# The pool's fp32 products replaced by products of rounded halves

## The chip, the cores and the metric

The kernel runs on one core of a Trainium2 chip. The metric is device time in microseconds of one execution, as the median of several. The engines named here are TensorE (PE; its weight loads are listed as PEld), VectorE (DVE), ScalarE (ACT) and SyncE (SP), which issues most transfers.

## What is computed

A decoder trunk of two residual layers on 256 tokens of 2048 features, all in float32. Layer 0 has a parallel attention and retention mixer, layer 1 a pooling mixer; each layer ends in a gated MLP with a short convolution, and a last norm follows. The change touches the pooling mixer of layer 1 alone:

```
h = rms_norm(x, mix_norm[1])
for group gi, window w in ((0, 2), (1, 4), (2, 8), (3, 16)):      # 512 channels each
    pooled_g[s] = mean(h_g[max(0, s-w+1) .. s]) - h_g[s]          # over min(s+1, w) tokens
    y_g = pooled_g @ pool_w[gi]                                   # 512 x 512
x = x + y * pool_scale
```

The trailing mean minus the token itself is a linear map over the 256 tokens, so it is a product with a fixed 256 x 256 matrix per group, the pool matrix. It is zero above the diagonal and more than w - 1 below it; only its first w columns (tokens that have fewer than w predecessors, the ramp) hold fractions other than 1/w; all the others hold 1/w and 1/w - 1, where w is a power of two.

## The kernel before

**Weight products.** Every weight matrix is streamed once from memory in units of 512 rows by 512 columns, four tiles of 128 rows each, into four slots `raw`. For accuracy a float32 product is made of three products of rounded halves: ScalarE writes the rounded value (`hi`, w_hi, L854), VectorE the remainder (`lo` = raw - hi, w_lo, L1265), and TensorE multiplies hi by the high half of the activation, lo by the same, and hi by the activation's low half (`token_unit`, L606, L608, L609). One unit is 24 products with 512 moving columns. `hi` and `lo` hold one unit, so ScalarE may round tile kt of the next unit only after TensorE is done with tile kt of this one (`w_used`), and a tile of `lo` follows its `hi` tile. The two elementwise engines have their other work written between these tiles by hand, at fixed places (`between`, called after each tile kt).

**The pool.** The map over tokens is applied after the channel product. TensorE takes units U_POOL + 0 to 3, one for each group; the result of group g, z_g, is 256 tokens (two tiles of 128 partitions) by 512 features in two PSUM banks. ScalarE copies it out and scales each token by its norm (`project_out`, L1091, one operation of 512 elements for each token tile, signal `z_ready`). Then `pool_tokens(g)` multiplies it by the pool matrix: for each of four blocks m of 128 features one fp32 product of token tile 0 with the first 128 + w columns of the matrix (L785), and one of token tile 1 with the last 128 (L787), both summed in the same two banks. VectorE adds the result times `pool_scale` to x (`pool_out`, L1693), in four operations. The tile of the matrix in SBUF, `pool_m`, has 384 columns for each group: 256 of the first 128 tokens, and 128 of the others.

**Order.** TensorE: units 0, 1, a small sum of squares (L622), unit 2, pool group 0, unit 3, pool groups 1 and 2, then the first up unit (`up`, first waits until `pool_out(1)` is done), pool group 3, the second up unit. ScalarE: hi of unit 1 with `last_squares` between (four `h` roundings, L860, at its end), hi of unit 2, the root of the squares, `project_out(0)`, hi of unit 3 with `project_out(1)` between, `project_out(2)`, hi of the first up unit with `first_h` between, `project_out(3)`, a square, then the `h` roundings of group 1 once `pool_out(1)` is done. VectorE: lo of unit 2, lo of unit 3, `pool_out(0)`, lo of the first up unit with the low half of `h` between (L1300), `pool_out(1)`, `pool_out(2)`, lo of the second up unit, `pool_out(3)`.

`z_of` (L191) gives the four groups' z the space of `yv`, `yg`, `u` and `yv` again, so `project_out(3)` waits for pool group 0 (`pooled_mm`). `act` (44 tiles by 512 elements, rounded type) holds the MLP's activations and isn't in use between the last down unit of layer 0 and the second window of the up products of layer 1.

Of the kernel before, what the change touches and what calls it, by code (L numbers as in the profile page):

```python
# [23 lines left out]
ALU = mybir.AluOpType  # L24
ACT = mybir.ActivationFunctionType
AX = mybir.AxisListType
F32 = mybir.dt.float32
F32R = mybir.dt.float32r

P = 128  # L30
# [5 lines left out]
KT = 4  # L36


def trunk_kernel(nc, xT, rel_bias, norm_g, w_in, w_out, lam, subln, pool_w, pool_scale,
                 w_up, conv, w_down, bucket_onehot, rot_cos, rot_sin, decay, pool_matrix, ident_in, flip_in, outT):  # L40
    D, S = xT.shape
# [80 lines left out]
    TURN = 32  # L122
    TAIL = 3
    NORM_AT = (1, 0)
    NEAR = [P + w for w in POOL_WINDOWS]

    ctx = ExitStack()
    with ctx:
# [59 lines left out]
        u = sb("u", [P, 4, S])  # L188
        yv = sb("yv", [P, 4, S])
        yg = sb("yg", [P, 4, S])  # L190
        z_of = [t.rearrange("p (t k) s -> p t (k s)", t=2) for t in (yv, yg, u, yv)]  # L191
        ps = ctx.enter_context(nc.psum_tensor("ps", [P, 8, 512], F32))

        def sem(name):
            return ctx.enter_context(nc.semaphore(name))
# [73 lines left out]
        gated = sem("gated")  # L269
        act_hi = sem("act_hi")  # L270
        act_lo = sem("act_lo")
        z_ready = sem("z_ready")
        pooled_mm = sem("pooled_mm")
        weighted = sem("weighted")
        x_rows = sem("x_rows")
# [211 lines left out]
        def _(pe):  # L487
# [286 lines left out]
            for l in range(DEPTH):  # L774
                if l == 1:
                    def pool_tokens(g):

                        pe.wait_ge(z_ready, 2 * (g + 1))
                        if g == 0:
                            pe.wait_ge(table_in, 16 * N_TABLE)  # L780
                        z, b = z_of[g], POOL_BANKS[g]
                        for m in range(4):
                            c = slice(m * P, (m + 1) * P)
                            out = ps[:, b + m // 2, (m % 2) * S:(m % 2 + 1) * S]
                            pe.matmul(out[:, 0:NEAR[g]], z[:, 0, c], pool_m[:, g, 0:NEAR[g]], start=m % 2 == 0, stop=False,  # L785
                                      skip_group_check=True)
                            mm = pe.matmul(out[:, P:2 * P], z[:, 1, c], pool_m[:, g, S:S + P], start=False, stop=True,  # L787
                                           skip_group_check=True)
                        mm.then_inc(pooled_mm, 1)

                    for g in range(4):
                        if g == 0:
                            pe.wait_ge(evacuated, G_POOL - 1)
                        if g == 2:
                            pe.wait_ge(evacuated, G_POOL)
                        if g == 3:
                            pe.wait_ge(rms_done, 3)

                        def pool_h(kt):
                            pe.wait_ge(h_lo, H_BASE[2] + KT * g + kt + 1)  # L800
                        token_unit(U_POOL + g, ps[:, POOL_BANKS[g]:POOL_BANKS[g] + 2, :], True, True, g, pool_h)
                        if g == 1:
                            sum_squares(2, POOL_BANKS[3] + 1)
                        if g >= 2:
                            pool_tokens(g - 2)
                    pool_tokens(2)

                def up(i, first):
                    for gt in range(2):
                        G = G_UP[l] + gt  # L810

                        pe.wait_ge(evacuated, i * 2 + G - (2 if first and gt == 0 and l == 1 else 1))
                        for j in range(UP_UNITS):
                            def split(kt):
                                pe.wait_ge(h_lo, H_BASE[2 * l + 1] + KT * j + kt + 1)
                            token_unit(U_UP[l] + 4 * gt + j, ps[:, wide_bank(G):wide_bank(G) + 2, :], j == 0,
                                       j == UP_UNITS - 1, j, split if first and gt == 0 else None, base=i * (8 * KT))
                            if first and l == 1 and gt == 0 and j == 0:
                                pool_tokens(3)
                            if first and gt == 1 and j == 0:  # L820
                                sum_squares(2 * l + 1, wide_bank(G_UP[l]) + 3)

                up(0, True)
                pe.wait_ge(rms_done, 2 * l + 2)
                with pe.Fori(1, PAIRS) as i:
                    up(i, False)
                for g in range(DN_GROUPS):
                    G = G_DN[l] + g
                    pe.wait_ge(evacuated, G - 1)
                    for j in range(DN_UNITS):  # L830
                        n, whole = U_DN[l] + DN_UNITS * g + j, j == DN_UNITS - 1
                        pe.wait_ge(act_lo, l * PAIRS + j + 1)
                        if l == 1 and g == DN_GROUPS - 1 and j == DN_UNITS - TAIL:
                            pe.wait_ge(act_lo, (l + 1) * PAIRS)
                            tail_units(n, ps[:, wide_bank(G):wide_bank(G) + 2, :], wide_bank(G + 1))
                            break
                        if l == 1 or g < DN_GROUPS - 1:
                            token_unit(n, ps[:, wide_bank(G):wide_bank(G) + 2, :], j == 0, whole, j, None, act)
                        else:
                            wide_unit(n, 0, wide_bank(G), j == 0, whole, lambda kt: act[:, KT * j + kt, :], None, opening(j))  # L840
# [3 lines left out]
        def _(sc_e):  # L844
# [238 lines left out]
            for l in range(DEPTH):  # L1083
                if l == 1:
                    def project_out(g, ts=range(2)):

                        sc_e.wait_ge(w_used, KT * (U_POOL + g + 1))
                        if g == 3:
                            sc_e.wait_ge(pooled_mm, 1)
                        for t in ts:  # L1090
                            a_.activation(z_of[g][:, t, :], ps[:, POOL_BANKS[g] + t, :], ACT.Copy,  # L1091
                                          scale=rstd[:, S + t:S + t + 1]).then_inc(z_ready, 1)

                    def last_squares(kt):
                        if kt == 1:
                            sc_e.wait_ge(evacuated, G_DN[0] + 4)
                            square(2, 3)
                        if kt == 3:
                            h_round(2, 3, 2)

                    def first_out(kt):
                        if kt == 0:
                            project_out(1, [0])
                        if kt == 1:
                            project_out(1, [1])

                    def first_h(kt):
                        if kt == 0:
                            sc_e.wait_ge(evacuated, G_POOL + 1)
                            h_round(3, 0, 3)  # L1110

                    w_hi(U_POOL, 0, 0, 16 * (R_POOL[0] + 1))
                    w_hi(U_POOL + 1, 0, 1, 16 * (R_POOL[1] + 1), last_squares)
                    w_hi(U_POOL + 2, 0, 2, 16 * (R_POOL[2] + 1))
                    root(2, POOL_BANKS[3] + 1)
                    sc_e.wait_ge(rstd_ready, 3)
                    project_out(0)
                    w_hi(U_POOL + 3, 0, 3, 16 * (R_POOL[3] + 1), first_out)
                    project_out(2)
# [140 lines left out]
        def _(ve):  # L1260
# [424 lines left out]
            for l in range(DEPTH):  # L1685
                if l == 1:
                    def pool_out(g):

                        ve.wait_ge(pooled_mm, g + 1)
                        b = POOL_BANKS[g]  # L1690
                        for m in range(4):
                            t = 4 * g + m
                            last = ve.scalar_tensor_tensor(x[:, t, :], ps[:, b + m // 2, (m % 2) * S:(m % 2 + 1) * S],  # L1693
                                                         pscale[:, t:t + 1], x[:, t, :], ALU.mult, ALU.add)
                        last.then_inc(evacuated, 1)

                    w_lo(U_POOL, 0, 0)
                    add_down(0, 3)
                    w_lo(U_POOL + 1, 0, 1, between=lambda kt: fold_last(kt - 1))
                    h_lo_group(2, 3, 2)  # L1700
                    w_lo(U_POOL + 2, 0, 2, kts=range(3))
                    invert(2)
                    w_lo(U_POOL + 2, 0, 2, kts=[3])
                    w_lo(U_POOL + 3, 0, 3)
                    pool_out(0)

                def v_windows(i, peel):
                    q = i * 2 + (l * 2 * PAIRS - 1)
                    for j in range(UP_UNITS):
# [6 lines left out]
                        if peel:  # L1716
                            if l == 0 and j == 0:
                                add_mixed(3)
                            if l == 0 and j == 3:
                                add_squares(1, 3)  # L1720
                            if l == 1 and j == 0:
                                pool_out(1)
                                pool_out(2)
                            if l == 1 and j == 1:
# [237 lines left out]
```

## Time and profile before

| | us |
|---|---|
| median of 3 runs | 1913.1 (1912.54 to 1913.1) |
| the profiled execution | 1912.37 |
| its span, first to last instruction | 1910.1 |
| TensorE busy in it | 1901.6 |
| VectorE busy | 1406.6 |
| ScalarE busy | 1064.0 |
| the pool's fp32 products, first to last start | 1166.97 to 1185.17 |

The times of the profile are microseconds from the start of the span. The granted TensorE clock is full throughout. A matmul's duration in the trace includes its way through the array, and consecutive ones overlap: what a product costs a busy TensorE is the distance between two starts.

### The profile page before, as it was taken

The page shows a single profiled execution, that of the slowest core. Times are in us where ns is not written, and L with a number is a line of the kernel's source. Part 1 is how long each engine was busy: PE and PEld are TensorE (multiplying, and loading weights), DVE is VectorE, ACT ScalarE, POOL GpSimd, SP SyncE. Part 2 cuts the span into 40 slices and gives each one's busy share as a digit, 9 for nine tenths or more (in the row PEclk, how much of TensorE's full clock was granted, in tenths as well). Part 3 has the DMA queues.
Part 4 walks back from the last instruction along what each step waited for, and adds up shares of the span by engine and source line. Part 5 has one row for each costly group of instructions (what it writes and reads, how often), then busy time and mean ns, then how long its engine had stood idle before and what let it go on. Part 6 is the DMA issues. An engine that isn't in the chain of part 4 may idle for free.

```text
span 1910.1 us, 26860 instructions
## 1 busy us (share of the span) xinstructions
PE 1901.6 (100%) x8654; PEld 1579.6 (83%) x8654; DVE 1406.6 (74%) x2287; ACT 1064.0 (56%) x1792; POOL 50.5 (3%) x54
## 2 busy tenths in 40 slices
PE   9999999999999999999999999999999999999998
PEld 8888888888888888888888888888888888888887
DVE  6666867777777777877766677777787777766665
ACT  7545544566555555555554556555555655555544
POOL 0000522000000000000000000000000000000000
PEclk9999999999999999999999999999999999999999
DMA  8845645575877777786665555677877777756653
GB/s 284 285 157 192 208 160 165 208 249 192 250 245 240 236 236 245 244 241 214 220 220 189 188 175 178 229 238 229 249 246 243 233 235 246 239 186 200 218 198 110
DMA packets 231984, 416.26 MB, mean 218 GB/s; under 512 B 13635, under 2 KB 54124, under 8 KB 231916
## 3 DMA queue, kind: packets, MB, share of 16 engines
q1 hardware_dynamic: 199804, 369.82, 59.4%
q10 hardware_dynamic: 32112, 45.55, 8.1%
q8 instruction: 41, 0.67, 0.2%
q14 instruction: 27, 0.22, 0.0%
HBM read 383.85 MB, written 24.13 MB: 214 GB/s over the span
## 4 chain that ended last, share of the span: by engine, by line
PE 98%; DVE 1%; ACT 0%; issue 0%; DVEq 0%
PE ps L606 29%; PE ps L609 29%; PE ps L608 29%; PE ps L498 4%; PE ps L502 2%; PE ps L570 1%; DVE lo L1265 0%; PE ps L585 0%; PE ps L574 0%; PE ps L589 0%; PE ps L593 0%; PE ps L541 0%; PE ps L543 0%; PE ps L542 0%; PE ps L720 0%; PE ps L785 0%
## 5 line engine op out<-in xcount | busy, mean ns | idle before, releaser
L1265 DVE TENSOR_TENSOR lo<-raw,hi 128x512 fp32r<-128x512 f32 x1352 | 919.6, 696 | 469.3 <-ACT hi L854 457.1
L854 ACT ACTIVATE hi<-raw 128x512 fp32r<-128x512 f32 x1336 | 830.8, 630 | 772.2 <-PE ps L609 706.4
L606 PE MATMUL ps<-hi,h 128*128 128x512 f32 x1824 | 714.8, 392 | 0.3 <-DVE lo L1265 0.2
L609 PE MATMUL ps<-hi,h 128*128 128x512 f32 x1824 | 710.3, 389 | 0.0
L608 PE MATMUL ps<-lo,h 128*128 128x512 f32 x1824 | 709.8, 389 | 0.0
L606 PEld LDWEIGHTS ps<-hi,h 128*128 128x128 f32 x1824 | 342.4, 188 | 74.6 <-DVE lo L1265 4.9
L609 PEld LDWEIGHTS ps<-hi,h 128*128 128x128 f32 x1824 | 342.3, 188 | 72.0
L608 PEld LDWEIGHTS ps<-lo,h 128*128 128x128 f32 x1824 | 342.5, 188 | 70.1
L606 PE MATMUL ps<-hi,act 128*128 128x512 f32 x592 | 230.5, 389 | 0.0
L609 PE MATMUL ps<-hi,act 128*128 128x512 f32 x592 | 230.3, 389 | 0.0
L608 PE MATMUL ps<-lo,act 128*128 128x512 f32 x592 | 230.3, 389 | 0.0
L606 PEld LDWEIGHTS ps<-hi,act 128*128 128x128 f32 x592 | 111.1, 188 | 23.5 <-issue 0.5
L609 PEld LDWEIGHTS ps<-hi,act 128*128 128x128 f32 x592 | 111.1, 188 | 23.2
L608 PEld LDWEIGHTS ps<-lo,act 128*128 128x128 f32 x592 | 111.1, 188 | 23.0
L1057 ACT ACTIVATE yg<-u,cw 128x256 f32<-128x256 f32 x88 | 52.0, 590 | 17.4 <-DVE u L1634 17.4
L498 PE MATMUL ps<-act,hi 128*128 128x512 f32 x176 | 60.8, 394 | 0.0
L1057 ACT ACTIVATE yv<-u,cw 128x256 f32<-128x256 f32 x88 | 51.9, 590 | 14.0 <-DVE u L1634 14.0
L1634 DVE TENSOR_TENSOR u<-sqacc,rstd 128x512 f32<-128x512 f32 x84 | 54.0, 684 | 0.0
L1623 DVE STREAM_TRANSPOSE sqt<-ps 128x1024 f32<-128x1024 f32 x42 | 52.2, 1243 | 0.0
L502 PE MATMUL ps<-act,lo 128*128 128x256 f32 x176 | 48.1, 277 | 0.0
L1878 POOL TENSOR_TENSOR x<-x,rstd 128x512 f32<-128x512 f32 x2 | 2.6, 1280 | 1606.7 <-ACT rstd L1239 1606.7
L1669 DVE STREAM_TRANSPOSE u<-ps 32x256 f32<-32x256 f32 x96 | 42.8, 446 | 2.9
(207 smaller groups left out, 1179.8 us busy)
## 6 DMA issues: line engine op xcount, KB each, us to landing
raw<-in_w_up SPq DMA_DIRECT2D x176, 1024.0 KB, 5.7
raw<-in_w_down SPq DMA_DIRECT2D x88, 1024.0 KB, 5.1
raw<-in_w_in SPq DMA_DIRECT2D x52, 1024.0 KB, 7.0
turned_rows<-sqt ACTq DMA_DIRECT2D x42, 512.0 KB, 5.9
sqacc<-turned_rows ACTq DMA_DIRECT2D x168, 128.0 KB, 6.1
raw<-in_w_out SPq DMA_DIRECT2D x16, 1024.0 KB, 7.4
raw<-in_w_in SPq DMA_DIRECT2D x16, 256.0 KB, 5.3
sqacc<-sqt SPq DMA_DIRECT2D x128, 32.0 KB, 1.9
```

Source lines behind the costliest of these rows:

```text
L498: pe.matmul(ps[:, bank + m, :], hi[:, kt, m * P:(m + 1) * P], mv, start=first and kt == 0, stop=False, skip_group_check=True)
L502: return pe.matmul(ps[:, bank + m, S:2 * S], lo[:, kt, m * P:(m + 1) * P], mv[:, 0:S], start=False, stop=last and kt == KT - 1, skip_group ...
L570: pe.matmul(acc[:, m, :], hi[:, kt, c], mv, start=first and kt == 0 and a == 0, stop=False, skip_group_check=True)
L606: pe.matmul(acc[:, t, :], xh, hi[:, kt, :], start=first and kt == 0, stop=False, skip_group_check=True)
L608: pe.matmul(acc[:, t, :], xh, lo[:, kt, :], start=False, stop=False, skip_group_check=True)
L609: mm = pe.matmul(acc[:, t, :], xl, hi[:, kt, :], start=False, stop=last and kt == KT - 1, skip_group_check=True)
L854: a_.activation(out[:, kt, :], raw[:, slot, kt, :], ACT.Copy).then_inc(hi_done, 1)
L1057: a_.activation(y[:, m, :], u[:, m, :], ACT.Identity, scale=cw[:, l, bass.ds(t, 1), 2], bias=cw[:, l, bass.ds(t, 1), 3]).then_inc(y0, 1)
L1265: ve.tensor_tensor(halves[1][:, kt, :], raw[:, slot, kt, :], halves[0][:, kt, :].bitcast(F32), ALU.subtract).then_inc(lo_done, 1)
L1623: ve.transpose(turned_u.rearrange("p (q k s) -> p q k s", q=4, k=8), rows).then_inc(evacuated, 1)
L1634: scaled = ve.tensor_tensor(out, quads, r, ALU.mult)
L1669: ve.transpose(cols, rows).then_inc(x_turned, 1)
```

## The change

The z of each group is split into rounded halves. ScalarE rounds z out of the bank into `z_hi` (same operation as before, other output type and place, signal `z_rounded`), and VectorE computes z - z_hi out of the same bank into `z_lo` (`project_low`, signal `z_ready`). The pool matrix is rounded as a whole into `pool_hi`; a remainder `pool_lo` is made for the first 16 columns of each group, the ramp. All four lie in `act`. Each of the four feature blocks then has five products of rounded operands instead of two of fp32: z_hi and z_lo by the near columns, z_hi by the ramp's remainder (16 columns), z_hi and z_lo by the far columns.

```diff
+    RAMP = max(POOL_WINDOWS)
-        z_of = [t.rearrange("p (t k) s -> p t (k s)", t=2) for t in (yv, yg, u, yv)]
+        z_hi = [act[:, 2 * g:2 * g + 2, :] for g in range(4)]
+        z_lo = [act[:, 8 + 2 * g:8 + 2 * g + 2, :] for g in range(4)]
+        pool_hi = act[:, 16:19, :].rearrange("p a b -> p (a b)").rearrange("p (g c) -> p g c", g=4)
+        pool_lo = act[:, 19, 0:4 * RAMP].rearrange("p (g c) -> p g c", g=4)
...
                         pe.wait_ge(z_ready, 2 * (g + 1))
                         if g == 0:
-                            pe.wait_ge(table_in, 16 * N_TABLE)
-                        z, b = z_of[g], POOL_BANKS[g]
+                            pe.wait_ge(pool_split, 1)
+                        zh, zl, b = z_hi[g], z_lo[g], POOL_BANKS[g]
                         for m in range(4):
...
-                            pe.matmul(out[:, 0:NEAR[g]], z[:, 0, c], pool_m[:, g, 0:NEAR[g]], start=m % 2 == 0, stop=False,
+                            pe.matmul(out[:, 0:NEAR[g]], zh[:, 0, c], pool_hi[:, g, 0:NEAR[g]], start=m % 2 == 0, stop=False,
                                       skip_group_check=True)
-                            mm = pe.matmul(out[:, P:2 * P], z[:, 1, c], pool_m[:, g, S:S + P], start=False, stop=True,
+                            pe.matmul(out[:, 0:NEAR[g]], zl[:, 0, c], pool_hi[:, g, 0:NEAR[g]], start=False, stop=False,
+                                      skip_group_check=True)
+                            pe.matmul(out[:, 0:RAMP], zh[:, 0, c], pool_lo[:, g, :], start=False, stop=False,
+                                      skip_group_check=True)
+                            pe.matmul(out[:, P:2 * P], zh[:, 1, c], pool_hi[:, g, S:S + P], start=False, stop=False,
+                                      skip_group_check=True)
+                            mm = pe.matmul(out[:, P:2 * P], zl[:, 1, c], pool_hi[:, g, S:S + P], start=False, stop=True,
                                            skip_group_check=True)
...
                     def project_out(g, ts=range(2)):
                         sc_e.wait_ge(w_used, KT * (U_POOL + g + 1))
-                        if g == 3:
-                            sc_e.wait_ge(pooled_mm, 1)
                         for t in ts:
-                            a_.activation(z_of[g][:, t, :], ps[:, POOL_BANKS[g] + t, :], ACT.Copy,
-                                          scale=rstd[:, S + t:S + t + 1]).then_inc(z_ready, 1)
+                            a_.activation(z_hi[g][:, t, :], ps[:, POOL_BANKS[g] + t, :], ACT.Copy,
+                                          scale=rstd[:, S + t:S + t + 1]).then_inc(z_rounded, 1)
...
                     w_hi(U_POOL + 1, 0, 1, 16 * (R_POOL[1] + 1), last_squares)
+                    sc_e.wait_ge(w_used, KT * U_POOL)
+                    a_.activation(pool_hi[:, :, :], pool_m[:, :, :], ACT.Copy).then_inc(pool_rounded, 1)
                     w_hi(U_POOL + 2, 0, 2, 16 * (R_POOL[2] + 1))
...
+                    def project_low(g, ts=range(2)):
+                        for t in ts:
+                            ve.wait_ge(z_rounded, 2 * g + t + 1)
+                            ve.scalar_tensor_tensor(z_lo[g][:, t, :], ps[:, POOL_BANKS[g] + t, :], rstd[:, S + t:S + t + 1],
+                                                    z_hi[g][:, t, :].bitcast(F32), ALU.mult, ALU.subtract
+                                                    ).then_inc(z_ready, 1)
...
                     w_lo(U_POOL + 2, 0, 2, kts=[3])
-                    w_lo(U_POOL + 3, 0, 3)
+                    ve.wait_ge(pool_rounded, 1)
+                    ve.tensor_tensor(pool_lo[:, :, :], pool_m[:, :, 0:RAMP], pool_hi[:, :, 0:RAMP].bitcast(F32),
+                                     ALU.subtract).then_inc(pool_split, 1)
+                    project_low(0)
+                    w_lo(U_POOL + 3, 0, 3, between=lambda kt: project_low(1, [kt - 2]) if kt > 1 else None)
                     pool_out(0)
+                    project_low(2)
...
                             if l == 1 and j == 0:
+                                project_low(3)
                                 pool_out(1)
                                 pool_out(2)
```

## Rows read from the trace of the kernel before

**Rows 1.** The page: busy time of TensorE, and the chain that ended last, by engine.
```profile
PE 1901.6 (100%) x8654; PEld 1579.6 (83%) x8654; DVE 1406.6 (74%) x2287; ACT 1064.0 (56%) x1792; POOL 50.5 (3%) x54
PE 98%; DVE 1%; ACT 0%; issue 0%; DVEq 0%
```

**Rows 2.** Timeline of TensorE: start, length, line, operands, count of records merged.
```profile
1147.71 0.39 PE L498 MATMUL ps<-act,hi 128*128 128x512 f32 x1
1149.79 0.39 PE L498 MATMUL ps<-act,hi 128*128 128x512 f32 x1
...
1166.97 0.38 PE L785 MATMUL ps<-pool_m,yv 128*128 128x130 f32 x2
1168.98 0.40 PE L608 MATMUL ps<-lo,h 128*128 128x512 f32 x1
1173.98 0.39 PE L609 MATMUL ps<-hi,h 128*128 128x512 f32 x1
1174.21 0.39 PE L785 MATMUL ps<-pool_m,yg 128*128 128x132 f32 x2
1176.00 0.40 PE L785 MATMUL ps<-pool_m,u 128*128 128x136 f32 x2
1177.60 0.38 PE L787 MATMUL ps<-pool_m,u 128*128 128x128 f32 x2
1178.25 0.40 PE L608 MATMUL ps<-lo,h 128*128 128x512 f32 x1
1183.53 0.41 PE L785 MATMUL ps<-pool_m,yv 128*128 128x144 f32 x2
1185.63 0.40 PE L608 MATMUL ps<-lo,h 128*128 128x512 f32 x1
```

**Rows 3.** Timeline of TensorE's weight loads around the sum of squares, 1160.3 to 1162.2.
```profile
1160.80 0.64 PEld L622 LDWEIGHTS ps<-ones,sqacc 128*128 128x128 f32 x4
1161.35 0.19 PEld L606 LDWEIGHTS ps<-hi,h 128*128 128x128 f32 x1
1161.46 0.19 PEld L608 LDWEIGHTS ps<-lo,h 128*128 128x128 f32 x1
1161.71 0.19 PEld L609 LDWEIGHTS ps<-hi,h 128*128 128x128 f32 x1
```

**Rows 4.** Timeline of ScalarE, 1148 to 1196; in brackets idle time before and releaser.
```profile
1154.24 1.06 ACT L889 ACTIVATE sqt<-x 128x1024 f32<-128x1024 f32 x1 [0.55 <-DVE x L1683]
1155.20 1.21 ACT L854 ACTIVATE hi<-raw 128x512 fp32r<-128x512 f32 x2
1156.32 1.70 ACT L860 ACTIVATE h<-x,gains 128x256 fp32r<-128x256 f32 x4
1157.92 1.21 ACT L854 ACTIVATE hi<-raw 128x512 fp32r<-128x512 f32 x2
...
1161.22 0.63 ACT L854 ACTIVATE hi<-raw 128x512 fp32r<-128x512 f32 x1 [0.73 <-PE ps L609]
...
1174.94 1.25 ACT L1091 ACTIVATE yv<-ps,rstd 128x512 f32<-128x512 f32 x2
...
1177.89 1.71 ACT L860 ACTIVATE h<-x,gains 128x256 fp32r<-128x256 f32 x4 [0.76 <-DVE x L1693]
```

**Rows 5.** Timeline of VectorE, 1148 to 1196.
```profile
1156.54 0.42 DVE L1291 TENSOR_TENSOR sqt<-sqt 128x256 f32<-128x256 f32 x1
...
1162.12 0.67 DVE L1265 TENSOR_TENSOR lo<-raw,hi 128x512 fp32r<-128x512 f32 x1
1164.05 0.69 DVE L1265 TENSOR_TENSOR lo<-raw,hi 128x512 fp32r<-128x512 f32 x1 [1.26 <-ACT hi L854]
...
1168.95 1.66 DVE L1693 SCALAR_TENSOR_TENSOR x<-ps,pscale,x 128x256 f32<-128x256 f32 x4 [0.43 <-PE ps L787]
...
1175.78 0.47 DVE L1300 SCALAR_TENSOR_TENSOR h<-x,gains,h 128x256 fp32r<-128x256 f32 x1
1176.20 1.66 DVE L1693 SCALAR_TENSOR_TENSOR x<-ps,pscale,x 128x256 f32<-128x256 f32 x4
```

More of the change, by code:

```diff
@@ L271, in trunk_kernel @@
         act_lo = sem("act_lo")
+        z_rounded = sem("z_rounded")
         z_ready = sem("z_ready")
+        pool_rounded = sem("pool_rounded")
+        pool_split = sem("pool_split")
         pooled_mm = sem("pooled_mm")
```

## The prediction

> **What bounds the kernel now.** I read the page's busy shares and its chain of waits first [rows 1]: TensorE is busy for 1901.6 of 1910.1 us and 98% of the chain that ended last is TensorE work. So a change counts by the TensorE time it adds or removes, and by whether it makes TensorE wait. Next, TensorE in order of time around the pool [rows 2]. A product of the four-group pool is one `matmul` in fp32 and stands in the trace as two records ("x2"). Group 0 runs from 1166.97; the second product of the following weight unit starts at 1168.98, so its first began to stream one interval (0.227, below) earlier, at 1168.755: group 0 holds TensorE for 1.785 us. Group 1: 1174.21 to 1176.00, 1.79 us. Group 2: eight starts from 1176.00 to 1177.60 are seven intervals of 0.2286, so it ends at 1177.83, 1.83 us. Group 3: 1183.53 to 1185.63 less 0.227, that is 1185.40, 1.87 us. Sum 7.275 us for 32 products. After group 2 the next unit's second product starts at 1178.25, its stream at 1178.02: TensorE stood still for 0.19 us. `up` waits there for `pool_out(1)`, which VectorE ran from 1176.20 for 1.66 us, to 1177.86 [rows 5]; the wait reaches TensorE 0.16 us later.
>
> **The price of a product in halves.** The new products have operands of rounded type (as all weight products have) with 128 to 144 moving columns, and 16 for the ramp. None so short is in the trace. What is there: 512 columns every 0.227 us (1168.98 to 1173.98, 22 intervals), and the pair of a 512 and a 256 column product every 0.347 (1147.71 to 1149.79, six pairs), so 0.119 for 256 [rows 2]. Both are columns over 2.4 GHz plus 0.013, so 128 would stream in 0.066: that is the lower end, if nothing else limits. The upper end is the fp32 product itself, 0.223 (1.785 / 8), if short rounded products get no faster path. What decides is the stationary operand: each product loads its own. Where the moving side is one column, in the sum of squares before unit 2, the loads show what they take alone [rows 3]: four of them end with one that starts at 1160.80 + 0.64 - 0.19 = 1161.25, then come the loads of two rounded products at 1161.35 and 1161.46. That is 0.10 to 0.11 apart, and 0.11 between the two rounded ones, with almost no streaming beside the first; the following load, behind a 512-column stream, comes 0.25 later. A load overlaps the stream before it, so a product costs the longer of 0.11 and its stream. I take 0.11 for all five kinds, also for the 16 columns of the ramp.
>
> Per group: four blocks by five products (near high, near low, ramp, far high, far low) = 20 products x 0.11 = 2.20 us, where eight fp32 products took about 1.8. Four groups: 80 x 0.11 = 8.80 against 7.275: **+1.53 us** of TensorE. Forty-eight more products, each cheaper by half only.
>
> Beside this rule of the trace stands one of the Trainium skill (TensorE: Matmul & The Clock Gate, section "Back-to-back issue gap"), which speaks for a shorter spacing: in a stream of load and product pairs with 128 columns it gives about 81 ns each. By it a group would be an estimated 1.62 us and the four 6.5. No row here has such a pair; the loads in [rows 3] are 0.10 to 0.11 apart, so I go by these.
>
> **ScalarE.** Added: `pool_hi`, one Copy of 4 x 384 = 1536 elements per partition. A 1024-element ScalarE operation occupies 0.96 (1154.24 to the next at 1155.20), a 512-element one 0.58, so 1536 is about 1.4 us [rows 4]. It stands between the `h` roundings that end at 1158.0 and the `hi` tiles of unit 2, from 1157.92 before. These move to 1159.3, 1159.9 and 1160.5; the fourth waits for TensorE until 1161.22 as before [rows 4]. VectorE's `lo` of the first tile then ends at about 1160.6, and unit 2 begins at 1161.38: hidden, by 0.7 us. If that cover were gone it would cost up to 1.4. The eight `z` copies stay as they are, into other memory; the wait of `project_out(3)` for `pooled_mm` goes, and is worth nothing: at 1174.94 pool group 0 had been done for 6 us.
>
> **VectorE.** Added: `pool_lo`, 64 elements, about 0.2, and eight subtractions of 512 elements out of the bank. The near rows are four `x<-ps` operations of 256 elements in 1.66 us, 0.40 apart, and a 512-element operation lasts 0.69 where a 256-element one lasts 0.42: 0.27 for 256 elements more, so about 0.66 each [rows 5]. Bounds 0.60 and 0.80 (twice 0.40). In sum 5.3 us, and where they stand decides:
> - `pool_lo` and `project_low(0)` follow the `lo` tile at 1162.12: 1162.8, then 1162.9 to 1164.25. They delay the first `lo` of unit 3 from 1164.05 to 1164.25; TensorE wants it at 1169.2. Group 0 starts on time at 1166.97.
> - `project_low(1)` goes between tiles at 1167.1 and 1168.5: free, wanted at 1174.6.
> - Group 0 now ends at 1169.17, so unit 3, the ScalarE tiles behind it and `pool_out(0)` (1168.95 before [rows 5], now 1169.37 to 1171.0) are 0.415 later. `project_low(2)` runs to 1172.3, and the four pairs of `lo` and `h` low half behind it catch up: the last one waits for ScalarE's fourth tile again and ends at 1176.6 instead of 1176.2.
> - `project_low(3)` stands ahead of `pool_out(1)`. Its inputs are ready at 1176.05 and 1176.6, it runs 1176.6 to 1177.92. Then `pool_out(1)`: 1177.92 to 1179.58, and 0.16 later, at 1179.74, TensorE may start the first `up` unit. TensorE itself is through with group 2 at 1174.625 + 4.40 = 1179.03. It stands still for 0.71 us, where it was 0.19: **+0.52 us**. Queued behind on VectorE: `pool_out(2)` until 1181.2, and on ScalarE the `h` roundings of group 1, from 1179.6 (1177.89 before) and then the tiles of the second `up` unit, from 1182.2; TensorE wants those at 1187.4, so they are free.
>
> Group 3 stands between `up` units 0 and 1, its `z_ready` came at 1177.9. Nothing later in the kernel is nearer to a limit than before, so the loss isn't given back: 1.53 + 0.52 = **+2.05 us**. The profiled execution took 1912.37, its span of 1910.1 and 2.27 around it; it would become 1914.4. The median of the three runs is 1913.1 (1912.54 to 1913.1), 0.7 above the profiled one: I forecast **1915.2**. That is 0.11%, less than the 0.2% (3.8 us) that a measurement of this kernel tells from no change.
>
> **The rivals.**
> A, short products stream freely (0.066, the ramp 0.02): a group is 16 x 0.066 + 4 x 0.02 = 1.14 us. For it: the law of the 512 and 256 rows. Against it: [rows 3]. It doesn't bring 4 x 0.67 = 2.7 us, because VectorE takes the place of TensorE: `pool_out(0)` can't start before `project_low(1)` is through at 1169.1, `project_low(2)` ends at 1172.0, the four pairs of 1.0 us run without a gap to 1176.06, `project_low(3)` to 1177.4, `pool_out(1)` to 1179.04. The first `up` unit starts at 1179.2 instead of 1178.02, +1.2, and group 3 gives 0.7 back: +0.5, 1913.6. (By the 81 ns of the skill's page the same chain holds, and group 3 gives 0.25 back: an estimate of 1914.0.)
> B, on the other side: rounded products under 256 columns run at the fp32 pace. For it: nothing in the trace is shorter than 256, exactly where the stream (0.119) meets the load (0.11), and the two differ by operand type only. Against it: there is one record per rounded product and two per fp32 product. A group is 16 x 0.223 + 4 x 0.11 = 4.0 us; TensorE is then the later one and the stall of 0.19 goes: 16.0 - 7.275 - 0.19 = +8.5, 1921.6, slower by 0.44%. It decides from 0.14 us a product on.
> C, load and stream of short products don't overlap: 0.11 + 0.066 = 0.176 and 0.13 for the ramp, 3.3 a group, 13.3 - 7.275 - 0.19 = +5.9, 1919.0. Against it: the fp32 records overlap their loads already.
> D, the forecast with the `pool_hi` copy uncovered, +1.4: 1916.6. Against it, 0.7 us of slack at the first tile and more at each later one.
>
> **How the numbers follow.** Forecast 0.62, A (with the 81 ns case) 0.14, B 0.11, C 0.07, D 0.06. Range: down past A and the spread of the runs, 1912.9; up past D and to C, 1919.3; left out are B and the edges, under 0.2. Slower by over 0.2%, beyond 1916.9: B, C and the edge of D and of the forecast (a subtraction of 0.80 adds 0.14 x 2 on the way to `pool_out(1)`), 0.20. Faster by over 0.2% needs -3.8, more than A's whole TensorE saving: 0.02. Within: 0.78.
>
> **What would show it.** The 80 products start 0.11 apart, whatever their columns; 0.066, 0.176 or 0.22 speaks for A, C, B. The groups take 2.2 us each. The stop before the first `up` unit is about 0.7 us and ends with `pool_out(1)`. The `pool_hi` row lies near 1158 to 1159.4 with no gap on TensorE at 1161.4. The subtractions take about 0.66 apart. It would be wrong if TensorE had a stop at group 0 or 1, waiting for `z_ready` or `pool_split`, or if the difference lay anywhere outside 1160 to 1190.

## The result, and the profile after

The changed kernel takes 1915.37 us as the median of 22 executions, beside 1912.89 of 22 of the kernel before: a ratio of 1.0015, with a 95% interval of 1.0009 to 1.0021. That is 2.5 us more: the interval excludes equality, the ratio lies inside the 0.2% that was set as the bound of "no change", and the interval's upper end just past it. The forecast was 1915.2.

The 22 executions stand in two groups: 13 from 1914.56 to 1915.45 (middle 1915.02), nine from 1916.37 to 1917.45 (middle 1916.70). The profiled one, 1916.78, is of the upper group; its span is 1914.5. A second profile of the same kernel, from the lower group, follows with the first experiment.

TensorE at the end of unit 2, in pool group 0 and behind it, as in [rows 2]. Each product is one record now, and its length is modelled; what counts is the distance from five products to the next five (0.50 for the first five of group 0, 0.56 for the next).

```profile
1167.35 0.39 PE L616 MATMUL ps<-hi,h 128*128 128x512 f32 x1
1167.58 0.22 PE L792 MATMUL ps<-act 128*128 128x130 f32 x1
1167.63 0.28 PE L794 MATMUL ps<-act 128*128 128x130 f32 x1
1167.75 0.22 PE L796 MATMUL ps<-act 128*128 128x16 f32 x1
1167.83 0.31 PE L798 MATMUL ps<-act 128*128 128x128 f32 x1
1167.97 0.27 PE L800 MATMUL ps<-act 128*128 128x128 f32 x1
1168.08 0.28 PE L792 MATMUL ps<-act 128*128 128x130 f32 x1
...
1170.04 0.40 PE L615 MATMUL ps<-lo,h 128*128 128x512 f32 x1
...
1175.26 0.22 PE L792 MATMUL ps<-act 128*128 128x132 f32 x1
1177.44 0.28 PE L792 MATMUL ps<-act 128*128 128x136 f32 x1
...
1179.56 0.28 PE L800 MATMUL ps<-act 128*128 128x128 f32 x1
1180.25 0.50 PE L613 MATMUL ps<-hi,h 128*128 128x512 f32 x1 [0.41 <-DVE x L1706]
1180.59 0.56 PE L615 MATMUL ps<-lo,h 128*128 128x512 f32 x1
1180.95 0.63 PE L616 MATMUL ps<-hi,h 128*128 128x512 f32 x1
1181.37 0.63 PE L613 MATMUL ps<-hi,h 128*128 128x512 f32 x1
...
1187.42 0.23 PE L792 MATMUL ps<-act 128*128 128x144 f32 x1
1189.89 0.40 PE L615 MATMUL ps<-lo,h 128*128 128x512 f32 x1
```

Read it as [rows 2] were read. Group 0 holds TensorE from 1167.58 to 1170.04 - 0.227 = 1169.81, group 1 from 1175.26 to 1177.44, group 2 to 1179.56 + 0.11 = 1179.67, group 3 from 1187.42 to 1189.66: 2.23 + 2.18 + 2.23 + 2.24 = 8.88 us, where it was 7.275. Then the stop, from 1179.67 to 1180.59 - 0.227 = 1180.36: 0.69 us, where it was 0.19. Then something that the forecast doesn't have: the products of the first up unit follow each other every 0.427 us instead of 0.227, from about 1181 to 1184, and the unit takes 1180.36 to 1187.42, 7.06 us; before it was 1178.02 to 1183.53, 5.51 us. The stretches of this profile say why (columns: stretch, its length, busy time of PE, PEld, DVE, ACT, POOL, granted clock, DMA share, GB/s):

```profile
1174.00:1179.00 5.00, 5.00 (x41) 4.77 (x40) 4.77 (x10) 3.47 (x6) 0.00 (x0) 1.00 0.18 38
1181.00:1184.00 3.00, 3.00 (x9) 2.33 (x8) 1.15 (x3) 2.51 (x5) 0.00 (x0) 0.50 0.09 34
1184.00:1187.00 3.00, 3.00 (x15) 2.47 (x14) 1.86 (x5) 1.77 (x4) 0.00 (x0) 0.99 0.00 0
```

The granted clock is 0.50 in 1181 to 1184: TensorE ran at 1.2 GHz instead of 2.4 right behind the thin products and the stop. So this execution lost 1.61 us to the products, 0.50 to the stop and 1.55 to the clock, 3.66 in all. The spans differ by 4.4. Of the rest, 0.61 is there before anything of the change has run: the small sum of squares ahead of unit 2 starts at 1161.63 where it was 1161.02, and VectorE is as much later at 1152.33, before the `pool_hi` copy. That is no effect of the change: in the traces of the twelve experiments below the same sum starts anywhere from 1160.88 to 1161.89, and the two that are the kernel before up to there have 1161.49 and 1161.89.

VectorE and ScalarE, which answer to [rows 4, 5]: `pool_hi` (L1126), the subtractions (L1714) and `pool_out` (L1706).

```profile
1158.53 1.47 ACT L1126 ACTIVATE act<-pool_m 128x1536 fp32r<-128x1536 f32 x1
1159.91 1.65 ACT L867 ACTIVATE hi<-raw 128x512 fp32r<-128x512 f32 x3
```
```profile
1160.55 1.89 DVE L1278 TENSOR_TENSOR lo<-raw,hi 128x512 fp32r<-128x512 f32 x3 [0.47 <-ACT hi L867]
...
1163.31 0.22 DVE L1726 TENSOR_TENSOR act<-pool_m,act 128x64 fp32r<-128x64 f32 x1
1163.56 1.41 DVE L1714 SCALAR_TENSOR_TENSOR act<-ps,rstd,act 128x512 fp32r<-128x512 f32 x2
...
1177.23 1.40 DVE L1714 SCALAR_TENSOR_TENSOR act<-ps,rstd,act 128x512 fp32r<-128x512 f32 x2
1178.55 3.21 DVE L1706 SCALAR_TENSOR_TENSOR x<-ps,pscale,x 128x256 f32<-128x256 f32 x8
```

The copy of 1536 elements holds ScalarE for 1.38 us. The tiles of `hi` behind it come late by that, and TensorE doesn't wait for them: the first `lo` tile of unit 2 is written from 1160.55 to about 1161.24, TensorE begins that unit at about 1162.1. Two subtractions take 1.32 from the first start to what follows, 0.66 each. `project_low(3)` stands from 1177.23 to 1178.55 ahead of `pool_out(1)`, which ends 1.66 later, at 1180.2; TensorE goes on at 1180.36.

### The profile page after: what moved, and what is told of

The parts are those of the page before. It is cut to its first block, busy times and chain, and to the rows that moved or that the text cites. A ratio compares the mean times of both kernels' runs of the same rounds, so it can differ in the third digit from the quotient of the medians.

```text
span 1914.5 us, 26901 instructions
## 1 busy us (share of the span) xinstructions
PE 1905.4 (100%) x8670; PEld 1583.1 (83%) x8670; DVE 1412.8 (74%) x2296; ACT 1065.2 (56%) x1793; POOL 50.4 (3%) x54
## 4 chain that ended last, share of the span: by engine, by line
PE 98%; DVE 1%; ACT 1%; issue 0%; DMA 0%; DVEq 0%; ACTq 0%
PE ps L613 29%; PE ps L616 29%; PE ps L615 29%; PE ps L505 4%; PE ps L509 2%; PE ps L577 1%; DVE lo L1278 1%; PE ps L592 0%; PE ps L596 0%; PE ps L581 0%; PE ps L600 0%; PE ps L548 0%; PE ps L550 0%; PE ps L549 0%; PE ps L645 0%; PE ps L712 0%
```

## The experiments

All times below are medians. The experiments ran in three sets, each beside the kernel before on the same chip: the first four, where the kernel before had 1912.95 (33 executions); the next four, 1912.93 (28); and the last three with the second run of the longer stop, 1913.27 (29). Theory 1 and theory 2 of the expectations are stated in the first of them. "Over before" is over the kernel before of the same set.

**The changed kernel again.** No edit.

> The changed kernel itself, run again beside the others for a direct comparison. Theory 1 (80 products at 0.11 us, and a stop of about 0.7 us before the first up unit behind project_low(3) and pool_out(1)): 2.0 to 2.8 us over the kernel before. Theory 2, to which its profile gave rise: in some executions TensorE's granted clock falls to 1.2 GHz for about 3.4 us after that stop, which adds another 1.7 us, so that the times come in two groups, near 1914.9 and near 1916.6.

1915.17 of 11, ratio 1.0012 (1.0003 to 1.0021), 2.2 over before. Nine executions from 1914.44 to 1915.42, two at 1916.23 and 1916.43: two groups again. Its profile is of the lower group. TensorE there, around the stop:

```profile
1179.44 0.28 PE L800 MATMUL ps<-act 128*128 128x128 f32 x1
1180.14 0.50 PE L613 MATMUL ps<-hi,h 128*128 128x512 f32 x1 [0.42 <-DVE x L1706]
1180.48 0.40 PE L615 MATMUL ps<-lo,h 128*128 128x512 f32 x1
1180.72 0.40 PE L616 MATMUL ps<-hi,h 128*128 128x512 f32 x1
```

The same stop (1179.55 to 1180.25, 0.70), and products every 0.23 behind it. So these two profiles differ by whether the clock falls behind the stop. For all other executions the record has only the mean granted clock of the whole, which such a fall takes to 0.999. It is 0.999 in ten of the eleven upper executions of the 33 and 1.000 in one (1916.51), which must be high for another reason. In 14 of the 22 lower ones it is 1.000; 0.998 or 0.999 in the other eight doesn't tell a fall here, because the clock is also low at the very end of the kernel (in this profile, whose mean is 0.998, in the last 6 us alone).

**Without the stop.**

```diff
-pe.wait_ge(evacuated, i * 2 + G - (2 if first and gt == 0 and l == 1 else 1))
+pe.wait_ge(evacuated, i * 2 + G - (3 if first and gt == 0 and l == 1 else 1))
```

> The changed kernel, with the first up unit waiting for pool_out(0) in place of pool_out(1); the banks it writes are group 0's. TensorE then doesn't stop between pool group 2 and the first up unit, and nothing else is touched. Theory 1: 0.7 us less than the lower group of the changed kernel, near 1914.3, that is 1.5 over before. Theory 2, the stop is what lets the clock fall: all executions in one group, so 1 to 1.5 less in the median of a sample with both. Rival (the thinly streaming products alone bring the clock down, whatever the stop): two groups again, 1.7 apart.

1914.23 of 11, ratio 1.0008 (0.9999 to 1.0017): 0.94 less than the changed kernel beside it, 0.8 less than that one's lower group. Ten executions lie from 1913.73 to 1914.72, one at 1915.75, whose mean granted clock is 1.000. In its profile the first up unit follows group 2 at once:

```profile
1179.01 0.28 PE L800 MATMUL ps<-act 128*128 128x128 f32 x1
1179.13 0.45 PE L613 MATMUL ps<-hi,h 128*128 128x512 f32 x1
1179.41 0.40 PE L615 MATMUL ps<-lo,h 128*128 128x512 f32 x1
```

**`project_low(3)` behind `pool_out(1)`.**

```diff
                             if l == 1 and j == 0:
-                                project_low(3)
                                 pool_out(1)
+                                project_low(3)
                                 pool_out(2)
```

> The changed kernel with project_low(3) behind pool_out(1) in VectorE's order; the wait of the first up unit as it was. If it is this order that makes the stop, pool_out(1) ends 1.3 us earlier, ahead of pool group 2's end, and the result is that of the relaxed wait: near 1914.3, one group. If the stop came from elsewhere (the later end of unit 3, the four lo and h pairs), some 0.2 to 0.7 us of it stays.

1914.24 of 11, ratio 1.0007 (0.9997 to 1.0016), all from 1913.72 to 1914.91. Its profile:

```profile
1177.74 1.66 DVE L1706 SCALAR_TENSOR_TENSOR x<-ps,pscale,x 128x256 f32<-128x256 f32 x4 [0.33 <-PE ps L800]
1179.32 1.40 DVE L1714 SCALAR_TENSOR_TENSOR act<-ps,rstd,act 128x512 fp32r<-128x512 f32 x2
```
```profile
1179.66 0.28 PE L800 MATMUL ps<-act 128*128 128x128 f32 x1
1179.78 0.45 PE L613 MATMUL ps<-hi,h 128*128 128x512 f32 x1
```

`pool_out(1)` now waits for TensorE and not the other way round, and the stop is gone. It was the place of two subtractions in VectorE's order that made it. What the two kernels without a stop have left over the kernel before, 1.3 us, is the products: 1.61 in the profile, less the 0.19 of the old stop, is 1.42.

**The kernel before with the relaxed wait.** The same edit of the wait, in the kernel before.

> The kernel before with the same relaxed wait alone. Theory 1: its stop of 0.19 us goes, 0.2 us less than before (1912.7), and the profile shows the first up unit right behind pool group 2. Rival (the 0.19 us is how rounded products start behind fp32 products, not a wait): nothing changes.

1912.95 of 11, equal to before (ratio 0.9999, 0.9990 to 1.0008). In the profile the 0.19 us are gone (group 2 ends at 1178.69, the next unit's stream starts at 1178.68), but 0.2 us is less than 11 executions tell; the median neither confirms it nor denies it.

**Without the ramp products.** The kernel without the stop, less these:

```diff
-pe.matmul(out[:, 0:RAMP], zh[:, 0, c], pool_lo[:, g, :], ...)
```

> The kernel without the stop (relaxed wait of the first up unit), and without the 16 products by the ramp's remainder; the pool's first 16 tokens then lose what rounding takes from fractions like 1/3. Theory 1, a product costs its weight load, 0.111 us, however few its columns: 16 x 0.111 = 1.78 us less, near 1912.5, and the groups take 1.78 us each. Rival, 16 columns cost what they stream (0.02 us): 0.3 us less, near 1913.9.

1912.66 of 11, 1.57 less than without the stop (1.64 less than the next kernel, of the same set), 0.27 less than before (ratio 1.0000, 0.9991 to 1.0009). Sixteen products of 16 columns cost nearly what theory 1 says (1.78), and five times what they would if streaming were their price. One block of group 2:

```profile
1176.87 0.28 PE L792 MATMUL ps<-act 128*128 128x136 f32 x1
1176.98 0.28 PE L794 MATMUL ps<-act 128*128 128x136 f32 x1
1177.10 0.27 PE L796 MATMUL ps<-act 128*128 128x128 f32 x1
1177.20 0.28 PE L798 MATMUL ps<-act 128*128 128x128 f32 x1
1177.32 0.28 PE L792 MATMUL ps<-act 128*128 128x136 f32 x1
```

Four products in 0.45, five took 0.56 (1178.56 to 1179.12 in the changed kernel's group 2).

**A ramp of 128 columns.**

```diff
-    RAMP = max(POOL_WINDOWS)
+    RAMP = P
```

> The kernel without the stop, with the remainder of the pool matrix kept for 128 columns in place of 16, so that all 80 products have 128 or more moving columns; VectorE's pool_lo has 512 elements in place of 64. Theory 1: the same time as with 16 columns (1914.2 within 0.3), because 128 columns stream in 0.066 us behind a load of 0.111. Rival, streams add to loads: 16 x 112 columns / 2.4 GHz = 0.75 us more, near 1915.0.

1914.30 of 11, ratio 1.0008 (0.9999 to 1.0017), where 16 columns gave 1914.23 in the set before. One of the 11 executions took 4091.77 us, the only one of its kind in the record; why isn't known, and the median doesn't depend on it. Eight times the columns cost nothing: in the profile the loads are 0.11 apart as before, and 16 x 112 more columns stream behind them.

**A longer stop behind thin products, twice.**

```diff
-pe.wait_ge(evacuated, i * 2 + G - (2 if first and gt == 0 and l == 1 else 1))
+pe.wait_ge(evacuated, i * 2 + G - 1)
```

> The changed kernel with a longer stop: the first up unit waits for pool_out(2) too. The stop grows from 0.7 to about 2.2 us behind the rounded products. Theory 2 (stop and thinly streaming products together let the clock fall): 1.6 us over the changed kernel's lower group for the stop, and in more executions than there another 1.7 us: two groups near 1916.6 and 1918.3, most in the upper. Rival (the falls have nothing to do with the stop): one in five to one in two in the upper group, as before.

> The changed kernel with the longer stop once more, for the counts. Theory 2: at least half of the executions near 1918.3 (clock at 1.2 GHz for a while behind the stop), against two of eleven behind fp32 products with a stop of the same length. Rival, the kinds of product don't matter: as few as there.

1918.56 of 6 (ratio 1.0033, 1.0021 to 1.0045) and 1918.10 of 7 (1.0028, 1.0016 to 1.0039). No execution of the 13 is near 1916.6; the lowest is 1917.61. The two profiles show the fall, for the others it is read from their times: without it they would lie near 1916.5 (the changed kernel's lower group and 1.5 for the longer stop). The first has a stop of 2.16 us and the low pace from the first product on:

```profile
1179.36 0.28 PE L800 MATMUL ps<-act 128*128 128x128 f32 x1
1181.63 0.63 PE L613 MATMUL ps<-hi,h 128*128 128x512 f32 x1 [2.00 <-DVE x L1706]
1182.06 0.63 PE L615 MATMUL ps<-lo,h 128*128 128x512 f32 x1
```

The second has a stop of 2.25 us, four products at the full pace behind it, and the low one from the fifth or sixth on:

```profile
1181.07 0.50 PE L613 MATMUL ps<-hi,h 128*128 128x512 f32 x1 [1.98 <-DVE x L1706]
...
1182.45 0.63 PE L616 MATMUL ps<-hi,h 128*128 128x512 f32 x1
```

**The same stop behind fp32 products.** The same edit in the kernel before.

> The kernel before with the same longer wait: a stop of about 2.0 us in place of 0.19, behind fp32 products, which keep the array streaming. In both theories 1.8 us more for the stop, near 1914.75. If the thin products are needed for the clock to fall, one group; if a stop of 2 us does it by itself, another 1.7 us in a part of the executions, near 1916.4.

1914.90 of 11, ratio 1.0010 (1.0001 to 1.0019): 1.97 over before. Nine executions lie from 1914.31 to 1915.02; their middle is 1.73 over before, which is the stop (from 1178.30 to 1180.32, 2.02 us where it was 0.19, 1.83 more). Two are at 1916.09 and 1916.49. The profiled one is the latter, and has the low clock too, from about the sixth product on:

```profile
1180.20 0.50 PE L606 MATMUL ps<-hi,h 128*128 128x512 f32 x1 [1.75 <-DVE x L1693]
1180.55 0.40 PE L608 MATMUL ps<-lo,h 128*128 128x512 f32 x1
...
1181.80 0.63 PE L606 MATMUL ps<-hi,h 128*128 128x512 f32 x1
```

So behind a stop of 2 us the clock falls in two of 11 executions after fp32 products (one seen in a profile, one by its time) and in all 13 after the rounded ones. Theory 2 is borne out: falls come with the stop, and more often with the rounded products before it; "at least half" was too timid. One difference is left untested: the stops behind the rounded products were 0.14 to 0.23 us longer than the one behind fp32 products.

**A ramp product with 32 stationary columns.**

```diff
-pe.matmul(out[:, 0:RAMP], zh[:, 0, c], pool_lo[:, g, :], ...)
+pe.matmul(out[0:TURN, 0:RAMP], zh[:, 0, m * P:m * P + TURN], pool_lo[:, g, :], ...)
```

> The kernel without the stop, in which the 16 ramp products load 32 of their block's 128 features as stationary columns; the ramp's remainder is left out for the other 96. Theory 1, the 0.111 us is the time of loading 128 stationary columns: 32 take about a quarter, 0.03, a ramp product costs 0.03 to 0.05 and the sum is 1.0 to 1.3 us less than without the stop (1914.2), near 1913.1. Rival, 0.111 is what any product costs that comes with a load, whatever its size: nothing changes, 1914.2.

1913.71 of 11, ratio 1.0003 (0.9994 to 1.0012). The kernel with all 128 columns that ran beside it (next) had 1914.56, so 0.85 less. Loads and what follows them, in its profile:

```profile
1175.53 0.19 PEld L794 LDWEIGHTS ps<-act 128*128 128x128 f32 x1
1175.64 0.11 PEld L796 LDWEIGHTS ps<-act 128*32 128x32 f32 x1
1175.70 0.19 PEld L798 LDWEIGHTS ps<-act 128*128 128x128 f32 x1
1175.81 0.19 PEld L800 LDWEIGHTS ps<-act 128*128 128x128 f32 x1
```

Behind a load of 128 columns the next comes 0.11 later, behind one of 32 columns 0.06. Neither the proportional price (0.03) nor the fixed one (0.11): the price of a thin product falls with its stationary columns, to something near 0.06. The Trainium skill (TensorE: Matmul & The Clock Gate, section "LDWEIGHTS (loading the stationary operand)") gives the number of stationary columns divided by 1.2 as a load's nanoseconds: an estimated 107 ns for 128 and 27 ns for 32. The trace's 0.11 agrees with the first, its 0.06 is twice the second. The same page of the Trainium skill, in "Wait — 56ns, not 53.3ns?", has about 62 ns of sequencer time for each matmul in one of its modes. The 0.06 is near that; which mode this chip runs no trace here shows, so what sets the 0.06 is open.

**Two products in a row with one stationary operand.** The ramp product moved ahead of the z_lo product.

> The kernel without the stop, with the ramp product moved next to the near product of the same high half, so that two products in a row have the same stationary operand. Theory 1: each product loads its own, 80 loads, nothing changes (1914.2 within 0.3). Rival, an equal stationary operand isn't loaded again: up to 16 x 0.09 = 1.4 us less.

1914.56 of 11, ratio 1.0005 (0.9996 to 1.0014). The profile has a load ahead of every product, 0.11 apart. Nothing is saved by the order.

**The whole result without ramp products.** The matrix's ramp columns are stored as multiples of 1/w, `pool_lo` goes, and VectorE corrects 64 results a group:

```diff
...
+ramp = ps[:, b:b + 2, :].rearrange("p a (h s) -> p (a h) s", h=2)[:, :, 0:RAMP]
+factors = pool_m[:, g, S + P:S + P + RAMP].unsqueeze(1).to_broadcast([P, 4, RAMP])
+ve.tensor_tensor(ramp, ramp, factors, ALU.mult).then_inc(pool_split, 1)
+ve.wait_ge(pool_split, g + 1)
...
```

> A version with the whole result and without the ramp products: the matrix's first w columns are held as multiples of 1/w, which the rounded type holds exactly, and VectorE multiplies the ramp's 16 results of each block by w/(s+1) in the bank, one operation of 64 elements a group, ahead of pool_out. 64 products of 0.111 us, no stop, pool_lo gone. Theory 1: as without the ramp, near 1912.7, level with the kernel before (16 loads of halves cost the same as 16 records of fp32). Rival: the four operations on the bank and their waits (0.3 to 0.4 each) come on the path of pool_out and stop TensorE again, up to 1 us more.

1912.78 of 11, beside 1913.27 of before; ratio 0.9999 (0.9990 to 1.0008). The correction takes 0.22 us and puts `pool_out` off by 0.26:

```profile
1178.39 0.22 DVE L1703 TENSOR_TENSOR ps<-ps,pool_m 128x64 f32<-128x64 f32 x1
1178.65 1.66 DVE L1707 SCALAR_TENSOR_TENSOR x<-ps,pscale,x 128x256 f32<-128x256 f32 x4
```

It is level with the kernel before and no faster. Of the versions tried that keep the whole result, this is the fastest in halves; that none could be faster with z as the stationary operand isn't shown.

## Why the prediction was right

**A product costs its load, 0.11 us: shown.** The forecast had 8.80 us, the profile 8.88; +1.53 forecast, +1.61 measured. That it is the load and not the stream is shown from three sides: 16 products of 16 columns are worth 1.57 us, eight times the columns are worth nothing, and fewer stationary columns make it cheaper. Rival A (free streams, 0.066), B (the fp32 pace, 0.22) and C (load and stream added, 0.176) each ask for another time of a group, 1.14, 4.0 and 3.3 us, and the groups take 2.18 to 2.24. The single starts are not 0.11 apart, as the prediction had it: behind the ramp's 16 columns the next product starts after 0.07 to 0.08, and the one behind that after 0.14 to 0.15. The loads are 0.11 apart. The Trainium skill's 81 ns (TensorE: Matmul & The Clock Gate, section "Back-to-back issue gap") isn't reached either: 0.111 here.

The row that decided this was a small one, the loads of a one-column fp32 product and of the two rounded products behind it in [rows 3]. Why the exchange doesn't win is a near equality of two prices that have different reasons. Two rounded products cost two loads, 0.22, whatever their columns: a group takes 2.23 us with 130 near columns and 2.24 with 144. The fp32 product, two records, costs 0.22 too, but by its columns: in the kernel before, a near and a far product take 0.44 with 130 near columns (1166.97 to 1167.41) and 0.46 with 144 (1183.53 to 1183.99), and a group 1.785 and 1.87.

```profile
1167.41 0.39 PE L785 MATMUL ps<-pool_m,yv 128*128 128x130 f32 x2
...
1183.99 0.41 PE L785 MATMUL ps<-pool_m,yv 128*128 128x144 f32 x2
```

That is 0.085 us for four times 14 columns, 1.5 ns a column. So at 128 to 144 columns the prices are within 0.02 us of each other: 64 rounded products make 7.1 us, where the fp32 ones took 7.275. What is lost is the ramp, 16 x 0.11. At 256 columns it would be otherwise: an estimated 0.4 for the fp32 product by that slope, against two times 0.119 [rows 2]. No run tried it.

**The stop, +0.52: shown.** Measured 0.69 for a forecast of 0.71. Both kernels without it, by a relaxed wait and by VectorE's order, are 0.93 to 0.94 below the changed kernel beside them: 0.8 of it against its lower group, where the stop is 0.70 in the profile, and the rest because the median of all includes the high executions. The steps on the way (0.66 for a subtraction, `pool_out(1)` 0.16 ahead of TensorE's start) are in the profile as forecast.

**`pool_hi` hidden, the wait for `pooled_mm` worth nothing.** The profile shows the copy where it was put, 1.38 us for 1.4, and no gap on TensorE ahead of unit 2 (rival D). No run tried it without its cover.

**What the forecast didn't have: the clock.** "Nothing later in the kernel is nearer to a limit than before, so the loss isn't given back" is true and left one thing out: the stop doesn't only cost itself. In 11 of the 33 executions of the changed kernel the time is another 1.5 us up. The one of them that was profiled has a clock of 1.2 GHz for about 3 us right behind the stop, and the mean clock of nine others agrees with such a fall. The median of 22, 1915.37, lies at the upper edge of the lower group, whose middle, 1915.02, is 2.13 over before, where +2.05 was forecast. So the mechanism and its size hold for that group. That the median of all came within 0.2 of the forecast is partly luck: the 2.05 was added to a median of three executions, 1913.1, where 22 gave 1912.89, and the median of two groups fell by chance on the edge of the lower one. The difference of the medians is 2.48. Had a few executions more fallen, the median would have been near 1916.4, still within the range, by a mechanism that it doesn't name.

**A sign that the prediction had named.** It would be wrong, it said, if the difference lay outside 1160 to 1190. In the profile 0.61 of the 4.4 us does lie ahead of 1160. The start of the sum of squares scatters by 1.0 us among traces of both kernels, so a single pair of profiles can't carry that sign; 3.66 lies inside 1160 to 1190, and 0.1 behind it.

**Open.** That the thin products raise the chance of the fall is shown at stops of 2.0 to 2.25 us (13 of 13 against 2 of 11), but for their small difference in length. At 0.7 us it is shown only that high executions go with the stop: 11 of 33 with it, one in 22 without (the relaxed wait and the order together). Rare high executions, 1.4 to 2.2 us over the median, occur in the other kernels without a stop and in the kernel before as well; several of them have a mean clock of 1.000, so they are no such falls, and what they are isn't known. Six of the 13 executions with the long stop are another 0.8 to 1.8 us above the middle of the rest. Their mean clock is 0.997, which a longer time at the low clock would fit; both profiles taken there are of the lower ones, so why isn't known.

## What to carry to other kernels

Where the stationary operand changes with every rounded product, and no more than 144 columns stream behind it, count loads, not columns: 0.11 us for 128 stationary columns. An fp32 product is paid by its columns. At 128 to 144 of them it costs nearly as much as two rounded ones, so the exchange gains nothing and any third product is pure loss. When work is added to an engine that isn't the bound, look for the one place where the bound engine waits for it, and put the addition behind what it waits for. And a stop of TensorE can cost more than itself: here 0.7 us of it went with another 1.5 in up to a third of the executions.

## What the runs showed of the hardware that was not expected

- The granted clock fell from 2.4 to 1.2 GHz behind a stop of only 0.7 us that followed 4.4 us of products with at most 136 moving columns at 0.11 us each; the products after it came 0.427 us apart instead of 0.227, and the unit took 7.06 us instead of 5.51 (the profile of the changed kernel).
- Behind fp32 products with the same columns, a stop of 2.0 us did the same in two of 11 executions only, one of them profiled; behind the rounded ones, stops of 2.16 and 2.25 us in all 13, two of them profiled.
- The price of an fp32 product with 130 to 144 moving columns rises with the columns, that of two rounded ones doesn't: groups of 1.785 to 1.87 us before, of 2.23 and 2.24 after.
- A thin product with 32 stationary columns costs 0.06 us, one with 128 costs 0.11 (loads 0.06 and 0.11 apart, 0.85 us less for 16 of them). With one stationary operand in two products in a row there are still two loads, 0.11 apart.
